# The last u panel of the attention stage, split in halves behind the turned probabilities of units 0 and 1

## The reference

```
h    = rms_norm(x, norm1) * (1 + scale1) + shift1
proj = h @ w_in                        # u, q, k, v, gates
y_pool = pool_mixer(u)                 # windowed means of u, then a 128x128 product per group
y_nsa  = nsa_mixer(q, k, v, gates)     # three attention branches, each a softmax, gated and added
x = x + gate1 * (concat(y_pool, y_nsa) @ w_out)
x = x + gate2 * (square(relu(h2 @ w_ff1)) @ w_ff2)
# shift, scale and gate come from  mod = silu(c) @ w_mod[l] + b_mod[l]
```

## Time and profile before

| | |
|---|---|
| median of 3 runs | 1426.65 us |
| the profiled execution | 1432.3 us, its span 1430.6 us |
| TensorE matmul busy | 1331.0 us (93%) |
| VectorE busy | 945.3 us (66%) |
| ScalarE busy | 637.0 us (45%) |
| GpSimd busy | 36.9 us (3%) |
| mean granted clock of TensorE | 0.911 of full speed |

### The profile page before, as it was taken

One profiled execution on the slowest core, in us unless ns is written; L12 is line 12 of the kernel. 1 busy time (PEld: TensorE's weight loads), 2 busy tenths in 40 slices (PEclk: granted clock), 3 DMA queues, 4 the chain that ended last, 5 costly groups with the idle time before them and its releaser, 6 DMA issues.

```text
span 1430.6 us, 21886 instructions
## 1 busy us (share of the span) xinstructions
PE 1331.0 (93%) x8766; PEld 1175.9 (82%) x8766; DVE 945.3 (66%) x1347; ACT 637.0 (45%) x985; POOL 36.9 (3%) x39
## 2 busy tenths in 40 slices
PE   6798989999999989999999999898879998799997
PEld 6775578999998754789999998788759998699996
DVE  5767845788766688357655846987785653665653
ACT  3533304444445433144444444448876731644442
POOL 1012000000000120000000000000000000000000
PEclk7798559999999885699999999899989999899999
DMA  9352522686754425146555553236664361465540
GB/s 386 134 205 89 179 86 89 245 313 257 271 176 152 185 65 216 43 167 217 185 176 188 219 208 144 88 123 224 222 199 160 135 208 58 149 207 192 186 147 30
DMA packets 43622, 247.69 MB, mean 173 GB/s; under 512 B 4160, under 2 KB 12368, under 8 KB 15520
## 3 DMA queue, kind: packets, MB, share of 16 engines
q1 hardware_dynamic: 43104, 244.57, 48.0%
q0 software_dynamic: 448, 2.14, 0.5%
HBM read 245.58 MB, written 1.11 MB: 172 GB/s over the span
## 4 chain that ended last, share of the span: by engine, by line
PE 70%; issue 11%; DVE 11%; ACT 3%; DMA 3%; POOL 1%; SPq 0%; POOLq 0%; DVEq 0%; ACTq 0%
PE bank L335 13%; PE bank L337 13%; PE bank L336 13%; PE bank L569 12%; PE bank L570 6%; PE bank L411 2%; DVE w_lo L330 2%; DVE arena L840 2%; DVE arena L1682 1%; PE bank L649 1%; PE bank L620 1%; DMA arena<-dscr 1%; PE bank L634 1%; DMA mixf<-dscr 1%; DVE arena L967 1%
## 5 line engine op out<-in xcount | busy, mean ns | idle before, releaser
L330 DVE TENSOR_TENSOR w_lo<-raw,w_hi 128x2048 fp32r<-128x2048 f32 x170 | 390.3, 2299 | 225.9 <-ACT w_hi L325 225.6
L325 ACT ACTIVATE w_hi<-raw 128x2048 fp32r<-128x2048 f32 x170 | 324.4, 1910 | 231.6 <-PE bank L337 123.9
L569 PE MATMUL bank<-act,w_hi 128*128 128x512 f32 x768 | 282.1, 408 | 11.8 <-DVE act L861 5.4
L335 PE MATMUL bank<-act,w_hi 128*128 128x256 f32 x800 | 239.0, 299 | 10.1 <-DVE act L861 7.0
L335 PE MATMUL bank<-ff_hi,w_hi 128*128 128x256 f32 (+1 forms) x816 | 231.5, 284 | 1.9 <-issue 1.0
L336 PE MATMUL bank<-act,w_hi 128*128 128x256 f32 x800 | 231.4, 289 | 0.0
L337 PE MATMUL bank<-act,w_lo 128*128 128x256 f32 x800 | 230.9, 289 | 0.0
L337 PE MATMUL bank<-ff_hi,w_lo 128*128 128x256 f32 (+1 forms) x816 | 230.7, 283 | 0.0
L336 PE MATMUL bank<-ff_lo,w_hi 128*128 128x256 f32 (+1 forms) x816 | 230.6, 283 | 0.0
L570 PE MATMUL bank<-act,w_lo 128*128 128x256 f32 x768 | 218.5, 284 | 0.0
L569 PEld LDWEIGHTS bank<-act,w_hi 128*128 128x128 f32 x768 | 147.1, 192 | 50.5 <-issue 10.8
(11 more groups left out here) (289 smaller groups left out, 1841.4 us busy)
## 6 DMA issues: line engine op xcount, KB each, us to landing
raw<-in_panels SPq DMA_DIRECT2D x170, 1024.0 KB, 4.9
arena<-in_modw SPq DMA_DIRECT2D x48, 1024.0 KB, 6.7
mixf<-dscr SPq DMA_DIRECT2D x8, 512.0 KB, 5.7
arena<-dscr SPq DMA_DIRECT2D x8, 512.0 KB, 4.9
mixf<-dscr SPq DMA_DIRECT2D x8, 256.0 KB, 6.2
arena<-dscr SPq DMA_DIRECT2D x8, 256.0 KB, 5.1
cst<-in_cst SPq DMA_DIRECT2D x1, 1250.5 KB, 7.6
arena<-in_x SPq DMA_DIRECT2D x1, 1024.0 KB, 5.0
```

What stands on the lines that cost most here:

```text
L325: nc.scalar.activation(w_hi[slot(k)][:, :], raw[:, k % RAW, :], ACT.Copy).then_inc(hi_done, 1)
L330: nc.vector.tensor_tensor(w_lo[slot(k)][:, :], raw[:, k % RAW, :], w_hi[slot(k)][:, :].bitcast(F32), ALU.subtract).then_inc(lo_done, 1)
L335: nc.tensor.matmul(o, wh, xh, start=start, stop=False, skip_group_check=skip)
L569: nc.tensor.matmul(bank[4 + c][:, :], wh[:, s:s + P], act2[:, kc, :, :], start=kc == 0, stop=False)
```

## The change

On TensorE the panel is no longer done between the scores of unit 1 and the loop. Its first half stands behind the transposes of unit 0 and its second half behind those of unit 1. On ScalarE the copy of `u` moves from ahead of the loop to unit 1, behind the exponentials of unit 3 and ahead of the split of panel 11.

```diff
-        def pe_panel(pe, m, k, o, xh, xl, arrive=None):
+        def pe_panel(pe, m, k, o, xh, xl, arrive=None, halves=(0, 1)):
...
-            for c in range(2):
+            for c in halves:
...
             pe_scores(pe, l, 1, True)
-            pe_gfree(pe, l, 7)
-            pe_used(pe, pe_panel(pe, m, L_U1, G(7), act_hi, act_lo))
-
             pe.wait_ge(modc_ready, 2 * l + 1)
             for i in range(8):
                 pe_turn(pe, l, i)
+                if i == 0:
+                    pe_gfree(pe, l, 7)
+                    pe_panel(pe, m, L_U1, G(7), act_hi, act_lo, halves=(0,))
+                if i == 1:
+                    pe_used(pe, pe_panel(pe, m, L_U1, G(7), act_hi, act_lo, halves=(1,)))
                 if i + 2 < 8:
...
             exponentials(0)
             exponentials(1)
-            used(L_U1)
-            link(nc.scalar.activation(ub[:, 2:4, 16:16 + T], G(7)[:, :].rearrange("p (b t) -> p b t", b=2), ACT.Copy))
-            act.sem_inc(gfree[1], 1)
-            act.sem_inc(u_copied, 2)
             for i in range(8):
                 act_pt(act, l, i)
                 if i + 2 < 8:
                     exponentials(i + 2)
                 if i == 1:
+                    used(L_U1)
+                    link(nc.scalar.activation(ub[:, 2:4, 16:16 + T], G(7)[:, :].rearrange("p (b t) -> p b t", b=2), ACT.Copy))
+                    act.sem_inc(gfree[1], 1)
+                    act.sem_inc(u_copied, 2)
                     split_hi(act, m, 11)
```

## The result

The changed kernel takes 1437.51 us (median of 16 runs, 1431.36 to 1440.82) against 1426.96 us (16 runs) of the kernel before on the same chip: a ratio of 1.0078, 95% interval 1.0062 to 1.0094, so 10.5 to 11 us slower. Forecast were 8 us. One percent is 14.3 us in what follows. The profiled execution took 1437.01 us (span 1435.3, granted clock 0.913), close to its median; that of the kernel before (1432.3 us, clock 0.911) turned out to be slower than most of its kind: over 29 later runs the kernel before had a median clock of 0.917 and a median time of 1425.28. The two profiles therefore differ by only 4.7 us where the medians differ by 10.5.

The account below looks back on a forecast made before the run. VectorE and TensorE were taken to set the pace by turns, TensorE at low clock in units 3 to 5. A delay of 4.0 us a layer, twice, 8 us on 1426.65, gave 1435 us; 8-in-10 range 1422 to 1447, own range 1430 to 1441.

Parts of the forecast that it names:

- 5.1 us a layer: Upper end of the forecast's own range: scaling of unit 3 at 6 us and the half panel at 5.1 us.
- Step 1 and 2: Softmax uncovered, TensorE idle 4.1 us, transposes 3.4 us earlier; halves before scores spend the early start, 0.3 us left.
- Step 3: Window sums move beside unit 3's scaling, stretching it to 5.2 us; unit 3's transposes 3.9 to 4.0 us late.
- ratio of 1.68: Modulation steps beside GpSimd's sums: 3.92 against 2.33 us, making the second modulation half of unit 1 take 4.7 us.
- Step 4: After unit 3's transposes TensorE works without a break at the lower clock, so the four microseconds stay.
- Overlap harmless: Rival, chance 0.20: GpSimd's sums do not slow VectorE at the new place; no gain, no loss, 1426 us.
- Clock stays up: Rival, chance 0.13: TensorE keeps 2.4 GHz in units 3 to 5, 6.0 us saved less 4.0 lost a layer; 1422 us.
- Clock late: Rival, chance 0.15: after the idle softmax the halves fail to lift TensorE's clock; 1453 us, or 1447 if half 0 alone fails.
- theory C: From the experiments' expectations: lays the loss to TensorE's clock and its idle time in the softmax alone.

Follow-up runs that it names:

- late sums: GpSimd's window sums wait for the eleventh of twelve modulation halves: on the kernel before 1419.59 us (0.9961), on the changed kernel 1426.08 us (1.0012).
- the halves behind the scores: Changed kernel with each half panel behind the scores of the same unit instead of ahead, sums not delayed: 1434.47 us, 1.0060.
- the late copy: Kernel before with only ScalarE's copy of u, and so the window sums, moved behind unit 3's exponentials; panel whole ahead of the loop: 1431.52 us, 1.0033.

## Why the prediction was right, and where it was not

**Right: direction, place and the events.** The forecast was 1435 (1422 to 1447), the result is 1437.5. Up to unit 3 the marks that it named are in the profile of the first layer: 4.1 us of idle TensorE, transposes of unit 0 at 114.8, the scaling of unit 3 over 4 us beside GpSimd, product 2 at 143.3 (143.4 named), transposes of unit 3 at 148.6 (148.5 named), 4.0 us late. The first half took 4.0 us and not 4.8 (from 117.4 to 121.4 in the trace), so the maxima of unit 2 and unit 3 and the sums came 1.2 to 1.3 us sooner than named. Two marks failed: the output panel (step 4 below), and the clock in units 3 to 5, 0.61, which the forecast itself had called a sign of being wrong if it stood well above 0.5. One bound does not follow from its terms: 5.1 us a layer on 1426.65 give 1437, and not the 1441 of its own range.

**Step 1 and 2, cover and halves: mis-sized.** The forecast let the 4.1 us of idle time and the halves be paid for by the earlier start, with 0.3 us left over, and put the whole 8 us on the overlap. In one execution's trace this even comes true (maxima of unit 3 at 132.3, against 133.84 before). But over many runs the order costs 0.51% with the sums out of the way, 0.26% without sums, each give or take 0.4%: 4 to 7 us where 0 was said. Of its parts the first half counts most, 12 us by the pair that moves it alone, and most of that goes with the lost cover; half 1 inside the loop costs nothing measurable against a whole panel ahead of it (0.9961 to 0.9928 with the sums late), and perhaps 0.4% against its place behind the scores. The reason for the size is only partly shown: in the change VectorE is busy 7.10 of 13.70 us from 119.30 on, and the kernel with half 0 ahead, half 1 behind the scores and late sums has its maxima of unit 3 6.6 us earlier (23.9 against 30.5 us behind the first score).

**Step 3, the overlap: right in kind, the term probably too large, and its ratio wrong.** Named were 4.0 us a layer, 8 in all; measured 4.7 in all by the copy alone (1.3 to 8.1, so 8 is at the edge) and 3.9 by the late sums. The ratio of 1.68 for modulation steps beside sums was too low: three took 5.58 us here against 2.33 alone, 2.4 times, which made the second modulation half longer. The row behind the 1.68 ran on to 131.52 while the sums ended at 130.19, so it mixed steps beside the sums with one behind them; the maxima came 1.3 us sooner than forecast, so that both errors cancelled at product 2. The two terms' errors, by the middle values 3 to 4 us too much for the overlap and 4 to 7 too little for the order, made up for each other in the sum as well. That the forecast met the time so closely is in part luck.

**Step 4, what follows: wrong in this execution.** The delay was to stay to the end; the output panel was to start 4.0 us late and started 1.7 late (210.12 less 1.03 is 209.1, against 207.4). In the second layer it started 1.2 late. What differs in the rows is the clock: the earlier trace rows had 0.51 for TensorE in units 3 to 5, busy without a break; after the change the same units ran at 0.61 and TensorE was busy 29.00 of 31.39 us. The forecast took the stretch of one execution for the kernel's own; how it runs in the other executions of the kernel before, no trace shows. The granted clock of whole executions points the same way: the median was 0.917 to 0.918 in the kernel before (0.911 in the one profiled), 0.911 after the change, 0.909 to 0.912 in the three experiments with the sums at or near the changed place, and 0.919 to 0.926 in the eight with the sums late or left out or with half 0 ahead. Within the runs of the kernel before, 0.001 of clock went with 0.7 us. By that the 0.006 to 0.007 that the change loses go with 4 to 5 of its 10.5 us. This is a correlation over whole executions; it does not say which comes first, and not whether the idle stretch at 137 to 149 us, where the granted clock was 0.61, is the cause.

**The rivals.** Overlap harmless (0.20): refuted, the late copy alone costs 0.33% (0.09 to 0.57) and the scaling went from 1.28 to 4.12. Clock stays up (0.13): the clock did rise in units 3 to 5, to 0.61 and not to 1.00, and 2.3 us of the 4.0 were given back in this execution. The rule of the Trainium skill, "TensorE: Matmul & The Clock Gate", section "HAM oscillation — how this bites in real kernels", which the forecast set beside it, lays a falling clock to waits for data. The trace agrees in one place: behind TensorE's wait of 4.98 us the product of unit 2 took 1.09 us, where that of unit 1 at 133.25 took 0.65. It does not settle the rest: the 11.90 us without a gap of the halves behind the scores ran at 0.52. Clock late (0.15): did not happen in the change, where 13.70 us from 119.30 ran at 0.99, but it did in that same experiment, and goes with the missing gain of its order.

The Trainium skill, "SBUF — State Buffer", section "Who interferes with whom", says of two instructions that contend that the one issued first holds the shared pair of ports to its end and the other waits in full. By that the cost is a wait added to an instruction and not one ratio, and the trace agrees in part: six scalings of 0.21 us each rose to 0.69 (4.12 / 6), modulation steps of 0.78 to 1.86, so two quite different ratios. The added wait is not one number either, 0.47 us for a scaling and 1.08 for a modulation step.

**Open:** how much of the order's cost is the idle softmax and how much the clock that goes with it (theory C's two parts); and the share of order and overlap, since 0.26% and 0.51% are one value within their errors.

## What to carry over

Before a filler is taken from a wait to fill a later gap, price the wait that it covered: here half a panel was enough cover, and taking that half away cost 12 us (give or take 5), while for the other half no place tried cost more than the errors. GpSimd's sums are better off at the tail of the stage than beside VectorE where it sets the pace; one wait on a semaphore was worth 0.4 to 0.8%. And before a stretch of low clock is built into a sum, compare the time and granted clock of the profiled execution with those of the other runs, and the two layers with each other.

## What the runs showed of the chip

- Beside GpSimd's tensor_tensor in float32, VectorE's two-operand steps (128x512) took 1.65 to 1.86 us each against 0.78 alone, six small scalings (128x128) 4.12 against 1.28, while copies from PSUM stayed at 0.41 to 0.42. GpSimd paid as well: its first sum (128x1024) took 2.16 us beside modulation steps against 1.89 in the earlier trace rows, all eight together 11.7 against 10.8.
- After the same 4 us pause the clock had come up within the first half panel when its 24 matmuls stood right behind the transposes (0.99 from 119.30), but was 0.52 over 11.90 us when scores stood between, though TensorE had no gap in either.
- In the late copy, units 1 and 2 ran without a gap at 0.50 in the first layer and at 1.00 in the second, and the transposes of unit 3 came 4.4 us apart.
- Units 3 to 5, with nearly the same instructions, ran at 0.51 (kernel before) and at 0.61 (after), and of the 4.0 us that unit 3 was late, 1.7 were left at the stage's end.
